# Where the next step's scores stand in the attention steps of a two-layer transformer kernel

## Chip, cores and metric

The kernel runs on one core of one Trainium2 chip. The metric is the device time of one execution in microseconds (us). The median of three runs is given, and beside it stands one profiled execution. TensorE is written PE in the profile, VectorE DVE, ScalarE ACT, GpSimd POOL and SyncE SP.

## The reference, cut to what matters

Two layers, each with four branches (windowed attention A, rotary attention B, differential attention C, a gated linear recurrence D) and a feed-forward part, are followed by a second block with its own sliding-window attention, a state space model and two more feed-forward parts. All is float32; 512 tokens and 16 meta tokens, width 1024. The branches that matter here:

```python
# kind A: windowed, 4 heads of 64, 2 key heads, block of 128 queries
s_b = einsum(qb, kb) * scale + head_bias(rel_b)          # up to 384 keys of the band
s_m = einsum(qb, km) * scale + head_bias(rel_m)          # the 16 meta tokens
p = softmax(concatenate([s_b, s_m, s_sink], axis=-1), axis=-1)
o = einsum(p_b, vb) + einsum(p_m, vm)
# kind B: rotary, all keys
s = where(key_ok, einsum(qblk, k) * scale, MASK_VALUE)   # q, k normalised and rotated
p = softmax(s, axis=-1)
o = einsum(p, v)
```

## The kernel before

**Steps.** The attention of a layer is one list of steps, `att`, in the order of kinds C, A, B. A step is one block of 128 query tokens (the last block of a layer-0 kind has the 16 meta tokens) and one of two pairs of heads. Layer 0 has ten steps of each kind, layer 1 has eight, as it drops the meta tokens' queries. A step of kind C has four cells (head and component), one of A or B has two cells, one for each head. Two successive steps (`i` 0 and 1) share a group, whose output is scaled and stored together. The second block has sixteen steps of kind W, also with two cells.

**What each engine does for one step.** PE: `scores` (L1214; for B and C also L1207, the meta tokens' scores, in PSUM bank 5), which write two PSUM banks per step, A and B in turn banks 0, 1 and 2, 3. DVE: `minima` (L2375) of the negated scores into SBUF, `meta_scores` (L2396). ACT: `exps` (L1816). PE: `turn_probs` for each of the two heads (L1241 for the blocks of 128 keys into bank 4, and with the first head L1238 for the meta tokens into bank 5). ACT: `copy_turned` (L1830, and L1833 for the meta tokens) from PSUM to SBUF. PE: `values` (L1267), in the second step of a group after a spread of the reciprocals (L1253). ACT: `copy_group` (L1839). DVE: `scaled` (L2441).

**The order on PE** is that of the function `attention`, and PE works in program order. In iteration n it takes the scores of step n, the values of step n-2, the first head's transposes of step n-1, then a projection piece if `fills_at` has one for this n, then the second head's transposes of step n-1. A piece (`fill_piece`, L1299 to L1307) is 24 matmuls of the layer's input projection, which use bank 7. Its weights are split into a high and a low part by ACT (L1739) and DVE (L2234) in earlier steps. In five steps from `turn_step` on, `turn_heads` (L1278) transposes the rotated heads of a tile, also in bank 7, behind the second head's transposes. In the second block (`gated=True`) the scores of step n+1 already stand between the piece of other work (`gated_step`) and the second head's transposes.

**Waits that matter.** `turn_probs(c, 0)` waits for both exponentials of the step, `turn_probs(c, 1)` for the copy of the first head's transposes (one bank serves both). `values` waits for the copy of both. `turn_heads` and the next `fill_piece` wait for the copy of the piece. `scores` of a step with meta scores (B, C) waits for the copy of the meta tokens' transposes before it and for DVE's reading of the meta scores before it:

```python
if bank_user(n):
    pe.wait_ge(S["att_min"], bank_user(n))
if c["marked"]:
    if n and att[n - 1]["metas0"]:
        pe.wait_ge(S["att_ptm"], att[n - 1]["metas0"])
```

**Around the steps.** ACT's order in a step is: first exponential, copy of the first head's transposes, copy of a group, second exponential, copy of the piece, copy of the second head's transposes, then weight splits. DVE's minima of step n wait for the second head's transposes of step n-2, whose buffer they write again. In the first steps of A, DVE and POOL also rotate the heads of kind B. From the seventh step of B on (`split_from`) ACT and DVE split the weights and inputs of the gated pieces that follow the attention (L1389 to L1391).

Of the kernel before, what the change touches and what calls it, by code (L numbers as in the profile page):

```python
# [248 lines left out]
def build(nc, ins, out_dram):  # L249
    with ExitStack() as ctx:  # L250
# [456 lines left out]
        att, groups = [], []  # L707
# [52 lines left out]
        for ly in layers:  # L760
            for kind in "CAB":
                first = len(att)
# [48 lines left out]
        def bank_of(c, g):  # L811

            return g if c["kind"] == "C" else 2 * (c["n"] % 2) + g

        def bank_user(n):

            k = n - 1 if n and "C" in (att[n]["kind"], att[n - 1]["kind"]) else n - 2
            return cell_end(k) if k >= 0 else 0
# [232 lines left out]
        def _(pe):  # L1051
# [144 lines left out]
            def scores(c):  # L1196
                n, rows = c["n"], c["rows"]
# [5 lines that stand above are left out]
                    if c["marked0"]:  # L1203
                        pe.wait_ge(S["att_meta"], c["marked0"])
                    q, k = (CQ, MKC) if c["kind"] == "C" else (BQ, MKB)
                    a = c["group"]["a"]
                    mm(PS[0:rows, 5, 256:256 + k.shape[1]], q[c["i"]][:, a:a + rows], k, start=True, stop=True)  # L1207
                for half in range(2):
                    for i in range(len(c["cells"][0]["scores"])):
                        for g, x in enumerate(c["cells"]):  # L1210
                            if x["head"] == half or c["kind"] != "C":
                                col, k = x["scores"][i]
                                if half == 0 or c["kind"] == "C":
                                    last = mm(PS[0:rows, bank_of(c, g), col:col + k.shape[1]], x["q"], k, start=True, stop=True)  # L1214
                    if c["kind"] == "C":
                        last.then_inc(S["att_scores"], 1)
                if c["kind"] != "C":
                    last.then_inc(S["att_scores"], 2)

            def turn_probs(c, j):  # L1220
                n, rows = c["n"], c["rows"]
                if c["kind"] == "C":
                    pe.wait_ge(S["att_mix"], c["mixed0"] + 2)
                else:
                    pe.wait_ge(S["att_exp"], c["cell0"] + (2 if c["metas"] else j + 1))
                if 2 * n + j:
                    pe.wait_ge(S["att_pt"], 2 * n + j)
                of = lambda i: SB[0:rows, c["kept"] + (2 * i if c["kind"] == "C" else i), :]
                if j == 0 and c["metas"]:
                    if c["metas0"]:  # L1230
                        pe.wait_ge(S["att_ptm"], c["metas0"])
                    seen = att[n + 1]["marked0"] + att[n + 1]["marked"] if n + 1 < len(att) else 0
                    if seen and n + 1 < made_scores[0]:
                        pe.wait_ge(S["att_meta"], seen)
                    elif c["marked0"] + c["marked"]:
                        pe.wait_ge(S["att_meta"], c["marked0"] + c["marked"])
                    for i in range(2):
                        turn(PS[0:META, 5, P * i:P * i + rows], of(i)[:, 0:META], ident[0:rows, 0:rows])  # L1238
                for b, (col, v) in enumerate(c["heads"][j]):
                    if v.shape[0] == P:  # L1240
                        last = turn(PS[:, 4, P * b:P * b + rows], of(j)[:, col:col + P], ident[0:rows, 0:rows])  # L1241
                last.then_inc(S["att_turned"], 1)

            def values(c):
                n, rows, g, i = c["n"], c["rows"], c["group"]["n"], c["i"]
                if i and g:
                    pe.wait_ge(S["y_ready"], g)
                if i:
                    pe.wait_ge(S["att_r"], n + 1)
                    for m in range(2):  # L1250
                        for j in range(2):
                            at = 4 * ((n - 1 + m) % 4) + (2 * j if c["kind"] == "C" else j)
                            last = mm(PS[64 * j:64 * j + 64, 6, 256 + P * m:256 + P * m + rows],  # L1253
                                      rcp[0:rows, at:at + 1].to_broadcast([rows, HD]), ident[0:rows, 0:rows],
                                      start=True, stop=True, skip_group_check=True)
                    last.then_inc(S["att_spread"], 1)
                elif g:
                    pe.wait_ge(S["y_ready"], g)
                pe.wait_ge(S["att_pt"], 2 * n + 2)
                if c["metas"]:  # L1260
                    pe.wait_ge(S["att_ptm"], c["metas0"] + 1)
                k = len(c["heads"][0])
                for b in range(k):
                    for j in range(2):
                        v = c["heads"][j][b][1]
                        x = PT[j][:, b, 0:rows] if v.shape[0] == P else PTM[:, j, 0:rows]
                        last = mm(PS[64 * j:64 * j + 64, 6, P * i:P * i + rows], v, x, start=b == 0, stop=b == k - 1,  # L1267
                                  skip_group_check=True)
                last.then_inc(S["att_pv"], 1)
# [15 lines left out]
            def fill_piece(f):  # L1285
                n = f["n"]
                if n:
                    pe.wait_ge(S["fill_read"], n)
                if heads_by[0]:
                    pe.wait_ge(S["b_heads_ready"], heads_by[0])  # L1290
                for ld in f["lds"]:
                    pe.wait_ge(S["w_low"], ld.s + 1)
                a, z = TILES[f["t"]] if f["tokens"] else f["cut"]
                for k in range(KT):
                    xh, xl = HR[:, k, a:z], UR[:, k, a:z]
                    if f["tokens"]:
                        wh, wl = (part(f["lds"][k // 4])[:, k % 4, :] for part in (high, low))
                        out = PS[0:z - a, 7, 0:CG]
                        mm(out, xh, wh, start=k == 0, stop=False)  # L1299
                        mm(out, xh, wl, start=False, stop=False)  # L1300
                        last = mm(out, xl, wh, start=False, stop=k == KT - 1)
                    else:
                        wh, wl = (part(f["lds"][0])[:, k, :] for part in (high, low))
                        out = PS[:, 7, 0:z - a]
                        mm(out, wh, xh, start=k == 0, stop=False)
                        mm(out, wh, xl, start=False, stop=False)
                        last = mm(out, wl, xh, start=False, stop=k == KT - 1)  # L1307
                last.then_inc(S["fill_full"], 1)
                filled_by[0] = n + 1

            made_scores = [0]
# [18 lines left out]
                    mean_tile(b2["n_ssm"], s - MEAN_AT)  # L1330

            def attention(first, end, turns=None, l=0, gated=False):
                if gated:
                    scores(att[first])
                for n in range(first, end + 2):
                    if n < end and not gated:
                        if n == turns:
                            pe.wait_ge(S["b_heads_ready"], NT * (l + 1))
                        scores(att[n])
                        made_scores[0] = n + 1  # L1340
                    if first <= n - 2:
                        values(att[n - 2])
                    if first <= n - 1 < end:
                        turn_probs(att[n - 1], 0)
                    for f in fills_at.get(n, ()) if n < end else ():
                        fill_piece(f)
                    if gated:
                        gated_step(n - first)
                        if n + 1 < end:
                            scores(att[n + 1])  # L1350
                    if first <= n - 1 < end:
                        turn_probs(att[n - 1], 1)
                    if turns and 0 <= n - layers[l]["turn_step"] < NT:
                        turn_heads(l, n - layers[l]["turn_step"])
# [1693 lines left out]
```

## Time and profile before

| | |
|---|---|
| median of three runs | 3123.15 us (3118.74 to 3124.94) |
| profiled execution, its own time | 3124.82 us |
| its span | 3122.8 us |
| PE busy | 3000.0 us, 96% |
| DVE, ACT, POOL busy | 1729.2, 1006.6, 216.9 us |
| mean granted clock of TensorE | 0.978 |
| chain that ended last | PE 89%, DVE 5%, ACT 4%, issue 2% |

The span is the profiled execution from its first to its last instruction. Busy time is what an engine's instructions cover. The chain that ended last is followed back from the last instruction, at each step to what released it; its shares say on which engine time is lost if something is added there. The granted clock is 1.00 when TensorE runs at 2.4 GHz and 0.50 when it runs at 1.2 GHz. Layer 0's kinds A and B lie from 178 to 301 us of the span, layer 1's from 1234 to 1352 us, the second block's attention from 2599 to 2660 us.

### The profile page before, as it was taken

The numbers are of one execution on the slowest core, as the hardware profiler recorded it, in microseconds if no ns is written. First come the engines' busy times: TensorE is split into PE (matmuls) and PEld (weight loads), VectorE is DVE, ScalarE is ACT, GpSimd is POOL, SyncE is SP. The second block draws the span as 40 slices with busy tenths as digits, with TensorE's granted clock in tenths as the row PEclk, the third lists the DMA queues.
The fourth block names the chain that finished last, engine by engine and source line by source line (L and its number), as shares of the span: only waits on it lengthen the run. The fifth ranks groups of instructions, "written<-read, shape, count | busy, mean of one in ns | idle before, by whom it ended". The sixth has DMA issues, their size and how long they took to land.

```text
span 3122.8 us, 51509 instructions
## 1 busy us (share of the span) xinstructions
PE 3000.0 (96%) x21594; PEld 2566.2 (82%) x21594; DVE 1729.2 (55%) x3294; ACT 1006.6 (32%) x1737; POOL 216.9 (7%) x446
## 2 busy tenths in 40 slices
PE   8999999999999999999999999999999899899997
PEld 7877998999999997789998888878888655578886
DVE  4564577457556436547755765657447454543334
ACT  4655232332112336532223222233222305432222
POOL 0130222000000100211210000000000000000000
PEclk9999999999999999989999999999999999999999
DMA  5201111235433321111223443422334311123232
GB/s 185 101 29 35 60 60 61 73 136 171 160 122 123 135 73 42 40 43 61 69 70 143 166 169 130 151 75 94 114 108 150 140 45 38 54 81 106 84 102 73
DMA packets 74494, 302.45 MB, mean 97 GB/s; under 512 B 10729, under 2 KB 11113, under 8 KB 69273
## 3 DMA queue, kind: packets, MB, share of 16 engines
q1 hardware_dynamic: 57880, 230.04, 21.5%
q0 software_dynamic: 16384, 69.13, 6.1%
q8 instruction: 172, 2.82, 0.4%
q14 instruction: 58, 0.47, 0.0%
HBM read 288.51 MB, written 14.63 MB: 97 GB/s over the span
## 4 chain that ended last, share of the span: by engine, by line
PE 89%; DVE 5%; ACT 4%; issue 2%; POOL 0%; DMA 0%; DVEq 0%; SPq 0%; ACTq 0%
PE acc L1066 18%; PE acc L1067 18%; PE acc L1068 18%; PE acc L1389 5%; PE acc L1390 5%; PE acc L1391 5%; PE acc L1085 2%; PE acc L1267 2%; PE acc L1214 1%; ACT temps L1816 1%; PE acc L1617 1%; PE acc L1241 1%; PE acc L1434 1%; PE acc L1455 1%; PE acc L1121 1%
## 5 line engine op out<-in xcount | busy, mean ns | idle before, releaser
L1067 PE MATMUL acc<-normed_r,toep_r 128*128 128x512 f32 (+1 forms) x1808 | 635.4, 351 | 0.0
L1739 ACT ACTIVATE toep_r<-ring 128x1024 fp32r<-128x1024 f32 (+2 forms) x340 | 392.9, 1157 | 695.8 <-PE acc L1068 676.0
L2234 DVE TENSOR_TENSOR ring_r<-ring,toep_r 128x1024 fp32r<-128x1024 f32 (+2 forms) x340 | 458.0, 1348 | 261.3 <-ACT toep_r L1739 261.0
L1067 PEld LDWEIGHTS acc<-normed_r,toep_r 128*128 128x128 f32 x1808 | 340.7, 188 | 45.4 <-issue 0.2
L1066 PE MATMUL acc<-mixed_r,toep_r 128*128 128x264 f32 (+1 forms) x1056 | 342.7, 325 | 0.7 <-DVE normed_r L2217 0.6
L1066 PE MATMUL acc<-work_r,toep_r 128*128 128x512 f32 (+1 forms) x988 | 341.7, 346 | 1.5 <-DVE ring_r L2234 1.4
L1068 PE MATMUL acc<-work_r,ring_r 128*128 128x512 f32 (+1 forms) x988 | 340.9, 345 | 0.0
L1068 PE MATMUL acc<-mixed_r,ring_r 128*128 128x264 f32 (+1 forms) x1056 | 338.8, 321 | 0.0
L1066 PE MATMUL acc<-temps_r,toep_r 128*128 128x512 f32 x752 | 297.6, 396 | 11.5 <-DVE normed_r L2220 8.8
L1067 PE MATMUL acc<-work_r,toep_r 128*128 128x512 f32 (+1 forms) x880 | 307.3, 349 | 0.0
L1389 PE MATMUL acc<-residual_r,toep_r 128*128 128x264 f32 (+1 forms) x1024 | 301.8, 295 | 3.7 <-ACT toep L1956 2.1
L1068 PE MATMUL acc<-temps_r,ring_r 128*128 128x512 f32 x752 | 295.0, 392 | 0.0
L1390 PE MATMUL acc<-normed_r,toep_r 128*128 128x264 f32 (+1 forms) x1024 | 293.1, 286 | 0.0
L1391 PE MATMUL acc<-residual_r,ring_r 128*128 128x264 f32 (+1 forms) x1024 | 291.9, 285 | 0.0
L1066 PEld LDWEIGHTS acc<-mixed_r,toep_r 128*128 128x128 f32 x1056 | 198.8, 188 | 15.9 <-issue 1.0
L1068 PEld LDWEIGHTS acc<-mixed_r,ring_r 128*128 128x128 f32 x1056 | 199.0, 188 | 15.5
L1066 PEld LDWEIGHTS acc<-work_r,toep_r 128*128 128x128 f32 x988 | 185.6, 188 | 26.3 <-issue 2.2
L1389 PEld LDWEIGHTS acc<-residual_r,toep_r 128*128 128x128 f32 x1024 | 196.4, 192 | 10.7 <-issue 2.5
L1068 PEld LDWEIGHTS acc<-work_r,ring_r 128*128 128x128 f32 x988 | 185.6, 188 | 23.9
L1390 PEld LDWEIGHTS acc<-normed_r,toep_r 128*128 128x128 f32 x1024 | 196.6, 192 | 1.7
L1391 PEld LDWEIGHTS acc<-residual_r,ring_r 128*128 128x128 f32 x1024 | 197.0, 192 | 0.0
L1066 PEld LDWEIGHTS acc<-temps_r,toep_r 128*128 128x128 f32 x752 | 141.8, 189 | 50.7 <-issue 11.9
(432 smaller groups left out, 5293.0 us busy)
## 6 DMA issues: line engine op xcount, KB each, us to landing
ring<-in_w_pair SPq DMA_DIRECT2D x176, 512.0 KB, 3.5
ring<-in_w_down SPq DMA_DIRECT2D x64, 704.0 KB, 4.1
ring<-in_w_gb SPq DMA_DIRECT2D x64, 640.0 KB, 3.9
extra<-in_w_ada POOLq DMA_DIRECT2D x18, 1024.0 KB, 5.9
toep<-in_w_ada POOLq DMA_DIRECT2D x18, 1024.0 KB, 6.2
ring<-in_w_tm SPq DMA_DIRECT2D x24, 512.0 KB, 4.3
ring<-in_w_out SPq DMA_DIRECT2D x24, 512.0 KB, 3.5
ring<-in_w_fm SPq DMA_DIRECT2D x20, 512.0 KB, 3.7
```

The source lines that it names most:

```text
L1066: mm(out, wh, xh[:, a:z], start=i == 0, stop=False)
L1067: mm(out, wh, xl[:, a:z], start=False, stop=False)
L1068: last = mm(out, wl, xh[:, a:z], start=False, stop=end)
L1085: last = mm(PB[j.buf][:, s, 0:z - a], (wh, wl, wh)[stage], (xh, xh, xl)[stage][:, a:z], start=stage == 0 and i == 0, stop=stage == 2 and i ...
L1121: last = mm(PB[j.buf][0:j.rows, s, 0:z - a], w, x[:, a:z], start=i == 0, stop=i == len(j.terms) - 1)
L1214: last = mm(PS[0:rows, bank_of(c, g), col:col + k.shape[1]], x["q"], k, start=True, stop=True)
L1267: last = mm(PS[64 * j:64 * j + 64, 6, P * i:P * i + rows], v, x, start=b == 0, stop=b == k - 1, skip_group_check=True)
L1389: mm(out, wh, xh[:, a:z], start=m == 0, stop=False)
L1390: mm(out, wh, xl[:, a:z], start=False, stop=False)
L1391: last = mm(out, wl, xh[:, a:z], start=False, stop=m == len(xs) - 1)
L1739: A(high(ld), slot(ld), ACT.Copy).then_inc(S["w_high"], 1)
L2234: V.tensor_tensor(low(ld), slot(ld), high(ld), ALU.subtract).then_inc(S["w_low"], 1)
```

## The change

For kinds A and B the scores of step n+1 are issued in iteration n, behind the projection piece and ahead of the second head's transposes of step n-1, whenever n and n+1 are of the same kind. The first step of each kind and every step of kind C keep their scores at the head of their own iteration. The second block's steps, all of one kind, get the order that they had. The counter `made_scores`, by which `turn_probs` tells whether the next step's meta scores have been issued, is now set in all stages. Only PE's order changes.

```diff
             def attention(first, end, turns=None, l=0, gated=False):
-                if gated:
-                    scores(att[first])
+                made_scores[0] = first
+
+                def next_scores(n):
+                    scores(att[n])
+                    made_scores[0] = n + 1
+
                 for n in range(first, end + 2):
-                    if n < end and not gated:
+                    if n < end and n >= made_scores[0]:
                         if n == turns:
                             pe.wait_ge(S["b_heads_ready"], NT * (l + 1))
-                        scores(att[n])
-                        made_scores[0] = n + 1
+                        next_scores(n)
+                    kinds = [att[m]["kind"] for m in range(n, min(n + 2, end))]
+                    paired = len(kinds) == 2 and kinds[0] == kinds[1]
                     if first <= n - 2:
                         values(att[n - 2])
                     if first <= n - 1 < end:
@@
                         fill_piece(f)
                     if gated:
                         gated_step(n - first)
-                        if n + 1 < end:
-                            scores(att[n + 1])
+                    if paired and kinds[0] != "C":
+                        next_scores(n + 1)
                     if first <= n - 1 < end:
                         turn_probs(att[n - 1], 1)
```

## Rows read from the trace of the kernel before

**Rows 1.** Windows: start:end, us, busy PE, PEld, DVE, ACT, POOL; clock, DMA.
```profile
179.50:237.20 57.70, 53.04 (x503) 42.51 (x501) 35.84 (x119) 29.84 (x106) 26.09 (x25) 0.94 0.10 35
237.20:301.40 64.20, 58.30 (x573) 45.32 (x572) 31.79 (x93) 40.68 (x100) 0.00 (x0) 1.00 0.13 42
...
2599.00:2660.00 61.00, 51.56 (x372) 27.24 (x360) 29.58 (x131) 41.06 (x135) 0.00 (x0) 1.00 0.11 36
```

**Rows 2.** Waits of PE, layer 0: kind A (179.5 to 237.2), then B.
```profile
PE acc L1241 <- ACT mixed L1830: 2.6, 4, 1.1
PE acc L1278 <- ACT work L1863: 1.2, 3, 0.6
...
PE acc L1278 <- ACT work L1867: 0.4, 1, 0.4
...
PE acc L1241 <- ACT mixed L1830: 3.9, 5, 1.5
```

**Rows 3.** Timeline, PE, second block: start, duration, line, shapes, idle before.
```profile
2630.68 0.44 PE L1241 MATMUL acc<-con,temps 128*128 128x128 f32 x2
2631.71 0.66 PE L1267 MATMUL acc<-mixed,work 128*64 128x128 f32 x8 [0.60 <-ACT mixed L1830]
...
2634.16 0.44 PE L1241 MATMUL acc<-con,temps 128*128 128x128 f32 x2
2634.52 0.66 PE L1253 MATMUL acc<-con,small 128*64 128x128 f32 x8
2635.07 0.33 PE L1267 MATMUL acc<-mixed,work 128*64 128x128 f32 x2
```

**Rows 4.** Timeline, layer 0, step B6: PE and ACT.
```profile
279.38 0.60 PE L1241 MATMUL acc<-con,temps 128*128 128x128 f32 x4
280.76 0.63 PE L1241 MATMUL acc<-con,temps 128*128 128x128 f32 x4 [0.78 <-ACT mixed L1830]
...
280.02 0.60 ACT L1830 ACTIVATE mixed<-acc 128x512 f32<-128x512 f32 x1
280.51 0.36 ACT L1833 ACTIVATE cross<-acc 16x256 f32<-16x256 f32 x1
...
281.50 0.57 ACT L1830 ACTIVATE mixed<-acc 128x512 f32<-128x512 f32 x1
281.97 2.41 ACT L1739 ACTIVATE toep_r<-ring 128x1280 fp32r<-128x1280 f32 x2
```

**Rows 5.** Timeline, PE, layer 0, from step B1's piece to B2's values.
```profile
248.39 0.60 PE L1241 MATMUL acc<-con,temps 128*128 128x128 f32 x4
248.82 0.31 PE L1207 MATMUL acc<-con,work 128*128 128x32 f32 x2
...
250.12 0.33 PE L1267 MATMUL acc<-mixed,work 128*64 128x128 f32 x2
```

**Rows 6.** Timeline, PE, layer 0, step A3.
```profile
198.74 0.49 PE L1241 MATMUL acc<-con,temps 128*128 128x128 f32 x3
199.90 0.52 PE L1241 MATMUL acc<-con,temps 128*128 128x128 f32 x3 [0.67 <-ACT mixed L1830]
200.35 0.29 PE L1214 MATMUL acc<-work 64*128 64x16 f32 x2
```

**Rows 7.** Timeline and window, layer 0, steps A0 and A1.
```profile
181.76 0.58 PE L1241 MATMUL acc<-con,temps 16*128 16x16 f32 x4 [1.07 <-ACT mixed L1830]
...
186.36 0.56 PE L1299 MATMUL acc<-toep_r,residual_r 128*128 128x256 f32 x1
...
182.91 2.35 DVE L2234 TENSOR_TENSOR ring_r<-ring,toep_r 128x1024 fp32r<-128x1024 f32 x2
...
181.70:188.10 6.40, 6.34 (x52) 5.50 (x53) 5.71 (x19) 2.64 (x11) 2.19 (x1) 0.50 0.02 8
```

**Rows 8.** Timeline, PE, layer 1, step A3: the rotated heads.
```profile
1262.30 0.52 PE L1278 MATMUL acc<-con,work 128*128 128x128 f32 x3 [0.24 <-ACT work L1863]
```

**Rows 9.** Timeline, DVE, layer 0, from step B7 to B8.
```profile
286.76 2.89 DVE L2234 TENSOR_TENSOR ring_r<-ring,toep_r 128x1280 fp32r<-128x1280 f32 x2
```

## The prediction, before the result was known

> **What bounds the kernel now.** I read the page first: TensorE is busy 96% of the span and holds 89% of the chain that ended last, so an edit of TensorE's order is paid where TensorE stands still. The change touches kinds A and B of both layers, four stretches of some 60 us each. In layer 0 TensorE is busy 53.0 of 57.7 us in A and 58.3 of 64.2 us in B [rows 1]: some 5 us of each is idle. Next I read who TensorE waits for in these two [rows 2]: in A, 2.6 us in four waits before transposes (L1241) for ScalarE's copy (L1830), and 1.2 and 0.4 us in four before the rotated heads (L1278) for the copy of a projection piece; in B, 3.9 us before L1241. Last comes the timeline, step by step. Below, "A3" is step 3 of kind A, counted from 0. An odd step has the spread of reciprocals (L1253) ahead of its values (L1267); an even step starts its values at once.
>
> **What moves.** In step n TensorE issues today: scores(n), values(n-2), first head's transposes of n-1, a projection piece in most steps, second head's transposes, in five steps the rotated heads. After: scores(n+1) stand behind the piece and ahead of the second head's transposes. No instruction is added or dropped, no DMA is touched. Kind C keeps its order, the first step of A and of B starts as today, and the second block's sixteen steps have this order already, so they stay.
>
> What the scores shielded changes sides. Today their 0.9 to 1.3 us lie between the second head's transposes and the next values, which wait until ScalarE has copied exactly those transposes out of PSUM. After, nothing lies there but, in odd steps, the spread, and in A5 to A9 the rotated heads of the step before.
>
> **The price of the uncovered copy.** The trace has it twice. (a) The second block, which has this order now [rows 3]: second head's transposes start at 2630.68, the values at 2631.71 after 0.60 us idle. That is 1.03 from start to start, against 0.36 where nothing waits (2634.16 to 2634.52). So +0.67 for two blocks in an even step. In the odd step 2634.16 to 2635.07 is 0.91, spread included: 0.1 shorter than 1.03, and less than 0.1 of wait is left beside the spread's 0.5. (b) Between the two heads of a step without a piece. Four blocks, kind B: 279.38 to 280.76 is 1.38 [rows 4], against 0.43 unwaited, 248.39 to 248.82 [rows 5]: +0.95. Three blocks, kind A: 198.74 to 199.90 is 1.16, against 0.45 from 199.90 to 200.35 [rows 6]: +0.71. An odd step loses the spread's 0.5 and the 0.1 from it: +0.34 for four blocks, +0.1 for three. The rotated heads, three more transposes, hide another 0.45: +0.26 for three blocks, +0.22 for two, nothing in odd steps.
>
> **Layer 0, kind A.** Lost: A2 0.67, A3 0.1, A4 0.71, A6 0.26, A8 0.22: 1.96 us. Won: about 1.1 us of scores now cover each of the eight waits of [rows 2], 2.6 + 1.2 + 0.4 = 4.2 us, of which 1.07 are in A0 (181.76) [rows 7]. A0's is not quite whole, for what is late next is the piece of A1, whose weights VectorE splits from 182.91 for 2.35 us, to some 185.2. With 0.14 us for the hand-over it can start at 185.35, against 186.36 now: 1.0. Net -2.1 us.
>
> **Layer 1, kind A** (eight steps, all with pieces). Lost: A1, whose values are kind C's with four blocks, 0.34; A2 0.67; A3 0.1; A4 and A6 0.26 each: 1.63. Won: the waits before the rotated heads of A3 to A6, four times 0.24, of which the first is in [rows 8]: 0.95. Net +0.7.
>
> **Kind B, each layer.** B0 to B5 have no idle time to win back: piece, transposes, scores, values follow without a gap [rows 5]. Lost: B2, B4, B6 0.95 each, B3, B5 0.34 each: 3.53 us. B1's values follow one or two blocks in an odd step: at most 0.1. From B6 on there is no piece. Its wait of 0.78 does not go away: the next scores write the bank in which the 16 meta tokens' transposes lie, and wait for their copy (L1833), which ends at 280.87, later than L1830's at 280.62 [rows 4]. So scores start at 281.01 where transposes start at 280.76 now, and take 1.3 us (248.82 to 250.12, [rows 5]). The second head's transposes end near 282.9, and their copy, at 281.50 now, starts 1.4 us later. Queued behind it on ScalarE without a gap are two weight splits of 2.41 us [rows 4] and the exponentials of B7. Behind those comes the copy of a pair, on which VectorE's scaling, its 2.89 us of splits and the minima of B8 hang [rows 9]. So the last steps end 1.4 to 1.5 us later. B of layer 0: 3.53 + 1.5 = 5.0. Layer 1 has one such step, with splits of the same length behind it: 3.53 + 0.1 + 1.4 = 5.0.
>
> **Sum:** -2.1 + 0.7 + 5.0 + 5.0 = +8.6 us. The profiled execution took 3124.82 us for a span of 3122.8, so it would take 3133.4 for 3131.4. It is 1.67 above the median of the three runs, 3123.15; on the median the sum gives 3131.8 us.
>
> **The clock** is the unknown. TensorE's granted clock is 0.50 (1.2 GHz) for 6.40 us from 181.7, 6.34 of them busy, behind the wait of 1.07 us [rows 7]; the same happens behind the last waits of both B kinds. Such a fall costs up to 3.2 us. In A0 the wait of 1.07 goes, but TensorE then stands 1.6 us for VectorE's splits. If the clock stays up there, the 2.75 us of the fall behind 185.35 cost nothing, and A wins up to 1.4 more, 3.5. If a whole fall starts there, it costs 1.8 more than now, and A wins 0.3. At the ends of the B kinds falls may come earlier, longer or not at all: some 3 us either way. I count all as they are.
> The Trainium skill ("TensorE: Matmul & The Clock Gate", section "A second HAM failure mode: psum-queue depth-cycling") says that frequent small idles between groups of matmuls, made by waits on PSUM, can make the clock oscillate. By that rule every B step, now with a wait of 0.3 to 0.9 us, would be in danger. In this trace it does not hold for waits of that size: the second block's steps have 0.6 us of idle every other step and a granted clock of 1.00 over 61 us [rows 1, 3].
>
> **Rivals.**
> 1. *The waits are hidden after all* (not slower by a measurable amount). For it: VectorE paces A1 and ScalarE the last B steps, so not every wait of TensorE adds up. With B's waits at the bare idle of 0.78 (odd 0.2), tails of 1.0 and A at -3.5, it is 2 x (2.74 + 1.0) + 0.7 - 3.5 = +4.7, and with one fall of the clock fewer about +2: 3125 to 3128. Against it: the start-to-start intervals, which are what the next work feels, are 0.2 us longer than the idle.
> 2. *The clock oscillates* (the page's rule as a mechanism here): two to five more falls of up to 3.2 us each, +15 to +25, 3138 to 3148. Against it stands the row of 61 us at 1.00.
> 3. *Faster*: the values hardly stall on the copy. Were the interval with four blocks 0.9 instead of 1.38 us, the even B steps would lose 0.47, the odd none, the tails 0.5 each and A nothing: 2.8 + 1.0 - 4.1 - 0.95 = -1.3. With the clock up in A0 and the falls at the ends of B gone, some -6.5: near 3116.5. It decides from a copy of 0.2 us, where the rows have 0.57 to 0.60 for four blocks. That the moved scores have no effect at all is excluded, since TensorE keeps the program's order.
>
> **Chances.** Forecast as summed 0.62; rival 1 0.22; rival 2 0.08; rival 3 0.08. 0.2% is 6.2 us, also the distance between the lowest and the highest run before, and about what a measurement of this kernel can tell from no change. So slower by more 0.70, within it 0.22, faster 0.08. The range goes from rival 1's lower part to rival 2's lower edge, 3125.5 to 3138.
>
> **What the profile after would show.** In B2, B4, B6 of both layers idle of some 0.8 us before L1267, released by L1830, in the odd ones 0.2 to 0.3. TensorE's waits for L1830 before L1267 5 to 7 us in the four stretches together, where there are none now. In A the waits before L1278 gone and before L1241 nearly so. The wait of B6 before L1207 instead of L1241. B with pieces 3.5 us longer per layer, its tail 1.5. The second block's stage unchanged. Wrong would be: no idle before L1267; a clock below 1.00 inside B0 to B6; or an A of layer 0 that ends over 3.5 us sooner.

## The result, and the profile of the changed kernel

The changed kernel took 3137.99 us (median of six runs, 3134.62 to 3140.26), the kernel before 3126.30 in six runs (3118.74 to 3129.91). The ratio is 1.004, with a 95% interval from 1.003 to 1.005: slower by 11.7 us by the medians (9.4 to 15.6 by the interval), where 8.6 were forecast. The profiled execution took 3140.13 us for a span of 3138.1, 15.3 more than before. On its page PE is busy 3010.4 us, 10.4 more than before, though it issues the same instructions: part of the loss is not waiting but slower work.

Lines behind the edited function have moved by 5 (L1830 is L1835, L1389 is L1394, L2234 is L2239). As in the prediction, a wait or a loss "in B2" is one in iteration B2, where the values of step B0 stand. The stretches below are named by steps: "B4's values", at which one ends, are the values of step B4, taken in iteration B6. Windows of the changed kernel, columns as in [rows 1]: layer 0's A, its B as far as B4's values, its tail of B (from there to the first gated piece), then the same three of layer 1.

```profile
180.10:237.70 57.60, 55.23 (x527) 43.55 (x525) 37.64 (x123) 31.10 (x110) 26.12 (x25) 0.94 0.11 38
237.70:281.90 44.20, 41.79 (x363) 33.02 (x362) 19.33 (x59) 25.47 (x62) 0.00 (x0) 1.00 0.17 57
281.90:312.80 30.90, 24.37 (x213) 16.15 (x213) 12.49 (x36) 15.72 (x40) 0.00 (x0) 0.72 0.02 6
1242.60:1300.50 57.90, 55.24 (x515) 44.42 (x513) 33.28 (x99) 30.51 (x95) 23.57 (x25) 1.00 0.11 39
1300.50:1346.20 45.70, 43.27 (x372) 33.76 (x372) 19.64 (x59) 25.72 (x59) 0.00 (x0) 1.00 0.16 54
1346.20:1368.10 21.90, 16.09 (x132) 11.32 (x132) 8.34 (x20) 11.28 (x25) 0.00 (x0) 0.75 0.02 8
```

The same six stretches of the kernel before, in one window each:

```profile
178.00:237.20 59.20, 54.54 (x527) 43.62 (x525) 37.04 (x123) 31.34 (x110) 26.09 (x25) 0.94 0.10 37
237.20:277.80 40.60, 40.59 (x363) 33.13 (x362) 18.70 (x56) 25.73 (x62) 0.00 (x0) 1.00 0.17 53
277.80:301.50 23.70, 17.72 (x215) 12.20 (x213) 13.14 (x38) 14.98 (x39) 0.00 (x0) 0.99 0.06 23
1234.10:1290.90 56.80, 54.37 (x515) 44.39 (x514) 32.57 (x99) 31.03 (x94) 23.61 (x25) 1.00 0.12 40
1290.90:1332.50 41.60, 41.60 (x372) 33.84 (x372) 19.01 (x56) 25.84 (x59) 0.00 (x0) 1.00 0.15 49
1332.50:1352.90 20.40, 15.71 (x135) 11.36 (x133) 9.02 (x23) 11.04 (x24) 0.00 (x0) 0.73 0.07 27
```

The differences, from the starts of the instructions at the borders (B4's values start at 277.77 before and at 281.88 after, and so on):

| stretch | forecast | measured in these two profiles |
|---|---|---|
| layer 0, A | -2.1 | -1.58 (59.19 to 57.61) |
| layer 0, B to B4's values | +3.5 | +3.61 (40.55 to 44.16) |
| layer 0, tail of B | +1.5 | +7.19 (23.72 to 30.91) |
| layer 1, A | +0.7 | +1.06 (56.83 to 57.89) |
| layer 1, B to B4's values | +3.6 | +4.05 (41.59 to 45.64) |
| layer 1, tail of B | +1.4 | +1.57 (20.37 to 21.94) |

That is +15.9. Of the rest of the span, the part ahead of layer 0's A is 2.08 longer and the part between the two layers' attention 2.71 shorter, and from layer 1's first gated piece to the end it is 1769.95 us before and 1769.98 after. Five of the six stretches came out within 0.6 us of the forecast. One did not, and its granted clock is 0.72 where it was 0.99. A low stretch of the clock stands at the border behind it in both profiles, so part of what this tail loses comes back in the 2.71 us.

The forecast waits, in PE's timeline of the changed kernel, layer 0, before the values of iteration B3 (odd) and of B4 (even), and the copy that releases the latter on ACT:

```profile
257.61 0.65 PE L1241 MATMUL acc<-con,temps 128*128 128x128 f32 x4
258.19 0.66 PE L1253 MATMUL acc<-con,small 128*64 128x128 f32 x8
258.95 1.09 PE L1267 MATMUL acc<-mixed,work 128*64 128x128 f32 x16
...
265.23 0.66 PE L1241 MATMUL acc<-con,temps 128*128 128x128 f32 x4
266.62 1.09 PE L1267 MATMUL acc<-mixed,work 128*64 128x128 f32 x16 [0.73 <-issue]
...
265.92 0.60 ACT L1835 ACTIVATE mixed<-acc 128x512 f32<-128x512 f32 x1 [1.39 <-PE acc L1241]
```

From start to start the even step takes 1.39 us (forecast 1.38), the odd one 1.34. The idle of 0.73 stands before the values in iterations B2, B4 and B6 of both layers. The profile puts it down to "issue", and one may think that it waits for nothing; but the copy of 0.60 ends at 266.52 and the values start 0.10 later. The doubled copy below settles it.

In layer 0's tail, PE and ACT of the changed kernel, and the window in which the clock is low:

```profile
285.08 0.38 PE L1207 MATMUL acc<-con,work 128*128 128x32 f32 x2 [0.99 <-issue]
...
291.60 0.22 PE L1207 MATMUL acc<-con,work 128*16 128x32 f32 x2 [1.60 <-issue]
...
293.01 1.11 PE L1241 MATMUL acc<-con,temps 128*128 128x128 f32 x4
294.86 1.97 PE L1267 MATMUL acc<-mixed,work 128*64 128x128 f32 x16 [0.73 <-issue]
...
287.63 2.42 ACT L1744 ACTIVATE toep_r<-ring 128x1280 fp32r<-128x1280 f32 x2
```

```profile
292.60:306.10 13.50, 11.78 (x70) 7.25 (x68) 7.31 (x18) 5.48 (x12) 0.00 (x0) 0.50 0.01 1
```

B6's wait stands before the meta scores (L1207), as forecast. B7's is 1.60 us, behind the two weight splits on ACT (2.42 us together). Within a microsecond of its end the granted clock falls to 0.50 (1.2 GHz) and stays there for 13.5 us, 11.8 of them busy: the four transposes take 1.11 us where they take 0.66 at 1.00, the values 1.97 where they take 1.09.

In layer 0's A two of the forecast's details are seen: the wait of A0 is gone, with the next piece waiting for VectorE instead, and the new waits of the even steps are there.

```profile
187.49 0.55 PE L1299 MATMUL acc<-toep_r,residual_r 128*128 128x256 f32 x1 [0.20 <-DVE ring_r L2239]
193.63 0.66 PE L1267 MATMUL acc<-mixed,work 128*64 128x128 f32 x8 [0.52 <-issue]
203.79 0.88 PE L1267 MATMUL acc<-mixed,work 128*64 128x128 f32 x12 [0.63 <-DVE mixed L2446]
```

### The profile page after: what moved, and what is told of

It reads as the page before. It is cut to its first block, busy times and chain, and to the rows that moved or that the text cites. A ratio compares the mean times of both kernels' runs of the same rounds, so it can differ in the third digit from the quotient of the medians.

```text
span 3138.1 us, 51509 instructions
## 1 busy us (share of the span) xinstructions
PE 3010.4 (96%) x21594; PEld 2569.0 (82%) x21594; DVE 1729.7 (55%) x3294; ACT 1006.7 (32%) x1737; POOL 217.2 (7%) x446
## 4 chain that ended last, share of the span: by engine, by line
PE 88%; DVE 5%; ACT 3%; issue 2%; DMA 1%; POOL 0%; SPq 0%; DVEq 0%; ACTq 0%
PE acc L1066 18%; PE acc L1067 18%; PE acc L1068 18%; PE acc L1394 5%; PE acc L1395 5%; PE acc L1396 5%; PE acc L1085 2%; PE acc L1267 2%; PE acc L1214 1%; PE acc L1241 1%; ACT temps L1821 1%; PE acc L1622 1%; PE acc L1439 1%; PE acc L1460 1%; PE acc L1121 1%
## 5 line engine op out<-in xcount | busy, mean ns | idle before, releaser
L2239 DVE TENSOR_TENSOR ring_r<-ring,toep_r 128x1024 fp32r<-128x1024 f32 (+2 forms) x340 | 457.8, 1347 | 261.4 <-ACT toep_r L1744 261.1
L1394 PE MATMUL acc<-residual_r,toep_r 128*128 128x264 f32 (+1 forms) x1024 | 301.3, 294 | 3.7 <-ACT toep L1961 2.1
L1066 PEld LDWEIGHTS acc<-mixed_r,toep_r 128*128 128x128 f32 x1056 | 198.8, 188 | 15.9 <-issue 1.0
L1394 PEld LDWEIGHTS acc<-residual_r,toep_r 128*128 128x128 f32 x1024 | 196.2, 192 | 10.7 <-issue 2.5
```

What stands on the lines that cost most here:

```text
L1066: mm(out, wh, xh[:, a:z], start=i == 0, stop=False)
L1394: mm(out, wh, xh[:, a:z], start=m == 0, stop=False)
L2239: V.tensor_tensor(low(ld), slot(ld), high(ld), ALU.subtract).then_inc(S["w_low"], 1)
```

## The experiments

### Where in the change the loss lies

Four kernels that move the scores in a part of the steps only. The edit is one line, the condition:

```diff
-                    if paired and kinds[0] != "C":
+                    if paired and kinds[0] in "AW":                              # a_only
+                    if paired and kinds[0] in "BW":                              # b_only
+                    if paired and (kinds[0] == "W" or kinds[0] == "B" and n in fills_at):      # b_pieces
+                    if paired and (kinds[0] == "W" or kinds[0] == "B" and n not in fills_at):  # b_tail
```

**Kind A alone.** 

> The moved scores in kind A alone, kind B in its old order. Theory (the edit is paid where TensorE waits for the copy of the second head's transposes): layer 0's A 1.6 us shorter than before and layer 1's A 1.1 us longer, as in the profile after; both B kinds at their old lengths of 64.3 and 62.0 us; in all -0.5 us, not to be told from before. Rival 1 (A's order changes what the clock does behind it, since B's tail in layer 0 comes at another moment): layer 0's tail (from B4's values to the first gated piece) well over its 23.7 us, up to 31, and +5 us or more in all. Rival 2 (the stretches are not independent: A's edit feeds on B's): layer 0's A at its old 59.2 us.

**Kind B alone.** 

> The moved scores in kind B alone, kind A in its old order. Theory: all of the loss lies here. Layer 0's B with pieces 3.6 us longer than before, layer 1's 4.05, layer 1's tail 1.6, layer 0's tail 7.2: 16.4 us, of which the pieces after layer 0's attention gave back 2.7 in the profile after, because a fall of the clock came earlier instead; so +12 to +16 us. Rival (the long tail of layer 0 was a chance of that one profile, not the order's): the tail 1.5 to 2 us longer than its 23.7, and +9 to +11 in all.

**Kind B, the iterations with a piece.** 

> The moved scores in kind B only in iterations that have a projection piece (B0 to B5); from B6 on, and in kind A, the old order. Theory (two separate costs, waits under the pieces and the tail): the stretch with pieces +3.6 and +4.0 us as after, the tails at their old 23.7 and 20.4 us: +7.6 us in all. Rival (the clock falls in the tail because of the waits that B1 to B6 collected before it, not because of the tail's own order): layer 0's tail is still some 5 us longer than before, +12 or more in all.

**Kind B, the iterations without.** 

> The complement: the moved scores in kind B only in iterations without a piece (B6 to B8); everything else in the old order. Theory: the stretch with pieces at its old 40.6 and 41.6 us, layer 0's tail 7.2 us longer with the granted clock at 0.50 inside it, layer 1's 1.6 longer; with 2.7 given back behind layer 0's, +6 us in all. Rival (the order costs the tails 1.5 us each and the clock in layer 0 falls for another reason): tails +1.5 each, the clock at 1.00 until the end of layer 0's tail, +3 in all.

Measured beside 27 runs of the kernel before (median 3126.39):

| kernel | median us | ratio (95%) | L0: A, B, tail | L1: A, B, tail |
|---|---|---|---|---|
| a_only | 3122.56 | 0.9992 (0.9983 to 1.0001) | 58.38, 40.55, 26.52 | 57.88, 41.59, 16.92 |
| b_only | 3134.82 | 1.0033 (1.0021 to 1.0046) | 60.58, 44.18, 25.81 | 56.84, 45.65, 20.90 |
| b_pieces | 3129.78 | 1.0016 (1.0007 to 1.0025) | 60.45, 44.17, 25.11 | 56.83, 45.66, 16.92 |
| b_tail | 3125.04 | 1.0000 (0.9991 to 1.0008) | 59.39, 40.56, 29.23 | 56.83, 41.59, 18.47 |

Four things follow. The loss lies in kind B. B with pieces is 44.17 and 45.66 us wherever its scores are moved, and 40.55 and 41.59 wherever not: this term belongs to the order, to 0.02 us. The tails don't behave so: with the same order they differ by up to 5 us, and with the old order layer 1's is 16.92, not the 20.37 of the first profile. Windows of the tails in a_only (layer 0, layer 1), then in b_tail:

```profile
278.10:304.60 26.50, 20.55 (x214) 14.15 (x212) 13.13 (x38) 14.97 (x39) 0.00 (x0) 0.85 0.06 22
1336.10:1353.10 17.00, 12.21 (x135) 8.64 (x133) 9.04 (x24) 11.04 (x24) 0.00 (x0) 1.00 0.09 34
```

```profile
280.80:310.10 29.30, 22.67 (x215) 15.31 (x213) 13.20 (x39) 15.39 (x40) 0.00 (x0) 0.79 0.05 20
1339.90:1358.30 18.40, 12.52 (x134) 8.56 (x132) 8.98 (x22) 11.08 (x23) 0.00 (x0) 1.00 0.08 30
```

The length follows the clock column. With the clock at 1.00 in both, layer 1's tail takes 16.92 in the old order and 18.47 in the new: the order's own price is 1.55 us. In layer 0, from B4's values to B9's, the kernel before takes 22.27 (277.77 to 300.04) and b_only 24.15 (282.94 to 307.09), both ahead of their fall of the clock: 1.9 us. The forecast had 1.4 and 1.5.

The fourth is that the parts do not add up. By the ratios b_pieces is 5.0 us slower (2.2 to 7.8), b_tail 0 (2.5 at most, where its expectation had 3 or 6), and b_only, which has both edits, 10.3 (6.6 to 14.4), as its rival had it: 9 to 11, with the long tail of layer 0 a chance of one profile. Inside layer 1's tail the clock stays at 1.00 in the one profile of b_pieces and the one of b_tail. It falls there in all six profiles of kernels in which all of B's scores are moved: b_only, the changed kernel twice, and three kernels further below. Such a tail takes 20.9 us or more, against 18.47. Of five profiles with all of B in the old order, two have such a fall too (the kernel before, and its doubled copy below). So the two parts together may bring on a fall that either alone does not. It is not shown: there is one profile of each part alone, and the intervals are so wide that the parts could still add up.

### Does the same program fall at the same place again?

Both kernels, unedited, were profiled once more.

**Before.** 

> The kernel before once more, for a second profile of the same program. Theory (the granted clock inside the tails differs from execution to execution, the waits don't): the stretches without a fall of the clock keep their lengths within 0.1 us (B with pieces 40.6 and 41.6), while the low stretches behind B7's wait of 1.5 us come at another moment or not at all, and a tail differs by 1 us or more from 23.7 or 20.4. Rival (the clock follows from the program): every low stretch of before is at its place again, both tails as they were within 0.2 us.

**Changed.** 

> The changed kernel once more, for a second profile. Theory: B with pieces again 44.2 and 45.6 us, waits of 0.73 us before the values of the even steps again; layer 0's tail not 30.9 us but between 25.3 (the clock at 1.00 throughout: 23.7 and the order's 1.5) and 31. Rival (the order fixes the clock): 30.9 us again, with the granted clock at 0.50 from B7's wait of 1.6 us on.

The kernel before took 3121.88 us, with layer 0's tail at 26.79 and layer 1's at 16.92, against 23.72 and 20.37 in its first profile. The changed kernel took 3135.67, its tails 26.07 and 21.94, against 30.91 and 21.94. B with pieces was 40.56 and 41.59, and 44.16 and 45.65. So the first theory held: the waits are the program's, while the place of a fall differs from one profile to the next, by 3 to 5 us of a tail's time. The two profiles of a kernel may come from different chips, so that a difference between chips is not excluded; but 17 executions of the kernel before on one chip, beside the second profiles, spread from 3119.49 to 3128.69 us. One part goes against the theory: layer 1's tail of the changed kernel came out the same twice. Tails of before's second profile, then of the changed kernel's:

```profile
279.70:306.50 26.80, 20.82 (x215) 14.24 (x213) 13.15 (x38) 15.12 (x39) 0.00 (x0) 0.83 0.06 22
1336.10:1353.10 17.00, 12.21 (x135) 8.63 (x133) 9.04 (x24) 11.03 (x24) 0.00 (x0) 1.00 0.08 33
```

```profile
280.60:306.70 26.10, 18.89 (x213) 12.70 (x213) 12.54 (x36) 15.67 (x40) 0.00 (x0) 0.96 0.02 8
1341.60:1363.60 22.00, 16.12 (x133) 11.40 (x133) 8.41 (x21) 11.38 (x25) 0.00 (x0) 0.75 0.03 9
```

The waits in layer 1's tail are alike where the clock is not. PE's timeline of the changed kernel's second profile, where it falls, and of b_tail, where it doesn't:

```profile
1351.68 0.63 PE L1241 MATMUL acc<-con,temps 128*128 128x128 f32 x4 [1.92 <-ACT mixed L1835]
1353.35 1.97 PE L1267 MATMUL acc<-mixed,work 128*64 128x128 f32 x16 [1.04 <-DVE mixed L2446]
```

```profile
1349.90 0.63 PE L1241 MATMUL acc<-con,temps 128*128 128x128 f32 x4 [1.91 <-ACT mixed L1835]
1351.57 1.09 PE L1267 MATMUL acc<-mixed,work 128*64 128x128 f32 x16 [1.04 <-DVE mixed L2446]
```

### Is the wait before the values the copy's?

ScalarE copies the second head's transposes of kind B twice, in either order:

```diff
+                if j and c["kind"] == "B":
+                    A(aside.rearrange(...)[:, 0:k, 0:rows], PS[:, 4, 0:P * k].rearrange(...)[:, :, 0:rows], ACT.Copy)
                 A(PT[j][:, 0:k, 0:rows], PS[:, 4, 0:P * k].rearrange(...)[:, :, 0:rows], ACT.Copy
                   ).then_inc(S["att_pt"], 1)
```

**In the old order.** 

> The kernel before; in kind B ScalarE copies the second head's transposes twice, the first time into a buffer that nobody reads, so the values are released 0.5 us later (0.49 from start to start of two such copies). Theory (in the old order the scores hide the copy): 1.73 us lie between the start of the transposes and the values where 1.38 are needed, so 0.15 us lost per even step and nothing per odd one; B with pieces 41.0 and 42.0 us. With the tails, where ScalarE is waited for, 1 to 1.5 us longer each, +3 to +4 in all. Rival (ScalarE's time per step is what paces B, the order beside the point): B with pieces some 3 us longer, as in the changed order.

**In the changed order.** 

> The same doubled copy in the changed order. Theory (nothing lies between the transposes and the values now): each of B2 to B6 loses the whole 0.5 us, 2.5 us in B with pieces, which is then 46.7 and 48.2 us, and the waits before the even steps' values grow from 0.73 to 1.2 us; tails 1 to 1.5 longer; +19 us or so against before, +7 to +8 against the changed kernel. Rival (the wait of 0.73 is not for the copy, since the profile names issue for it and not ScalarE): the wait stays 0.73 and the stretch 44.2 us.

In the old order B with pieces was 40.87 and 41.92 us, 0.3 more than before, and the whole 3127.08 (ratio 1.0003, 0.9994 to 1.0013; 3 to 4 us more were expected). In the changed order it was 46.61 and 48.09, 2.45 more than in the changed kernel, and the whole 3142.22 (1.0053, 1.0038 to 1.0068), 15.6 by the medians where 19 were expected. That is 3.9 more than the changed kernel's 11.7, where 7 to 8 were expected and the two stretches alone make 4.9; the whole is no sharper than that. PE and ACT in the changed order, layer 0 (lines moved by one):

```profile
266.93 1.09 PE L1268 MATMUL acc<-mixed,work 128*64 128x128 f32 x16 [1.22 <-issue]
275.01 1.09 PE L1268 MATMUL acc<-mixed,work 128*64 128x128 f32 x16 [0.59 <-ACT mixed L1838]
...
265.75 0.60 ACT L1837 ACTIVATE aside<-acc 128x512 f32<-128x512 f32 x1 [1.40 <-PE acc L1242]
266.24 0.59 ACT L1838 ACTIVATE mixed<-acc 128x512 f32<-128x512 f32 x1
```

The copy is 0.49 later, and the even step's idle grows from 0.73 to 1.22, by 0.49, though it is still called "issue". The odd step now shows 0.59 with the right name. This is the mechanism, shown from both sides: the order, and not ScalarE's time, decides what a copy costs in B with pieces.

### Does the spread of an odd step cover the copy?

```diff
+                    if paired and (kinds[0] == "W" or kinds[0] == "B" and n in fills_at and att[n]["i"] == 0):
```

> The moved scores only in the iterations B0, B2 and B4 of kind B; the values that follow them belong to odd steps and have the spread of the reciprocals ahead; kind A and everything else in the old order. Theory (the spread covers 0.6 of the 0.95 us, as the prediction had it): B1 at most 0.1, B3 and B5 0.34 each: B with pieces +0.7 to +0.8 us, 41.3 and 42.4 us, and the three uneven iterations hold the other 2.8 of the 3.6; within 0.2% of before, +1.5. Rival (each moved step costs the same): +1.8 per layer, 42.4 and 43.4.

B with pieces came out at 41.32 and 42.80: +0.77 and +1.21. The whole took 3123.91 (0.9997, 0.9988 to 1.0006). In layer 1, B3 and B5 cost 0.40 and 0.42 (from values to values: 7.18 to 7.58, 7.17 to 7.59), B1 0.20, and each even step 0.07, which no view explains. B3's pair, in the kernel before and in this one:

```profile
1304.82 1.09 PE L1267 MATMUL acc<-mixed,work 128*64 128x128 f32 x16
1312.00 1.04 PE L1267 MATMUL acc<-mixed,work 128*64 128x128 f32 x16
```

```profile
1305.99 1.09 PE L1267 MATMUL acc<-mixed,work 128*64 128x128 f32 x16
1313.57 1.09 PE L1267 MATMUL acc<-mixed,work 128*64 128x128 f32 x16
```

So the first theory held, with 0.41 where 0.34 was forecast. In the changed kernel an even step costs 1.02 (6.65 to 7.67).

### Can the clock be held up by filling the gaps?

Transposes of the identity go into bank 7, which is idle there, in the changed order. The function is shown without its calls: the first kernel calls it before the values and before the scores in B6 to B9, the second before the values of the even iterations and before the scores in B6 to B9.

```diff
+                def keep_busy(n):
+                    if att[n]["kind"] == "B" and n not in fills_at:    # busy_b: without the second condition
+                        pe.wait_ge(S["fill_read"], filled_by[0])
+                        for b in range(4):
+                            turn(PS[:, 7, P * b:P * b + P], ident, ident)
```

**In the tails.** 

> The changed order, and in the iterations B6 to B9 of both layers four transposes of the identity into the idle bank 7 before the values and four before the scores, 0.6 us of PE work at each place, laid into the gaps. Theory (the falls in the tails come from the gaps there, and PE is not what the tail waits for): the clock stays at 1.00 in both tails, layer 0's tail 25 to 27 us, layer 1's 18.5 to 20; against the changed kernel some -4 us or more, so +5 to +9 against before. Rival 1 (the clock falls for what went before, the pieces): falls in the tails as in the changed kernel, tails as long or up to 4 us longer, +12 to +16. Rival 2 (PE is the tail's bound, the added work is paid in full): each tail 8 times 0.5 = 4 us longer at a clock of 1.00.

**And before the values of every even step of B.** 

> The changed order, with four transposes of the identity into bank 7 before the values of every even step of kind B, whose gap of 0.73 us they fill to 0.3, and before the scores in B6 to B9. Theory (layer 1's tail falls to the clock of 0.50 because of the waits under the pieces and in the tail together, since with either alone it stayed at 1.00): with the gaps under the pieces filled too, layer 1's tail has no fall and takes 18.5 us, not 21.9; B with pieces as in the changed kernel, 44.2 and 45.6; +7 to +9 us against before. Rival (such filling does nothing for the clock, the pieces of idle left suffice, or it is chance): layer 1's tail 21.9 us again with the clock at 0.50 for 13.7 us.

The first took 3134.39 us (1.0028, 1.0016 to 1.0040), the second 3134.59 (1.0027, 1.0017 to 1.0037), 9.7 and 8.0 us over the kernel before by the medians, against the changed kernel's 11.7, but the intervals overlap. Layer 0's tails were 25.74 and 26.23 with a clock of 0.99 and 0.96. Layer 1's was 21.94 in both, as in the changed kernel, in spite of some 1.0 us more PE work; its windows, first kernel and second:

```profile
1343.30:1365.30 22.00, 17.24 (x145) 12.74 (x145) 8.42 (x21) 11.38 (x25) 0.00 (x0) 0.75 0.03 10
```

```profile
1342.40:1364.40 22.00, 16.99 (x141) 12.26 (x141) 8.41 (x21) 11.38 (x25) 0.00 (x0) 0.75 0.03 11
```

So in these profiles the theory of each expectation fell in layer 1. Waits of 1.36 and 1.04 us (first kernel), 1.48 and 1.04 (second) were left there in the iteration behind B6, and the clock fell during the latter, as in the changed kernel. In the first kernel:

```profile
1353.37 0.63 PE L1241 MATMUL acc<-con,temps 128*128 128x128 f32 x4 [1.36 <-ACT mixed L1845]
1355.03 1.97 PE L1267 MATMUL acc<-mixed,work 128*64 128x128 f32 x16 [1.04 <-DVE mixed L2456]
```

This profile is that of the slowest of the first kernel's seven executions, 3137.02 us. Three of them took 3126.59, 3127.05 and 3129.78, each below all seven of the changed kernel's (3134.62 at the least). What the clock did in those three no profile shows, so it is not settled that such filling in the tails gains nothing.

That PE is not the tail's bound is seen in layer 0, whose 25.74 with 28 more transposes stand beside b_only's 25.81. Rival 2 falls with that. What makes the clock fall in layer 1 stays open.

### A version that beats both

The moved scores in A's even iterations alone, where the values that follow have the spread ahead of them.

```diff
+                    if paired and (kinds[0] == "W" or kinds[0] == "A" and att[n]["i"] == 0):
```

> The moved scores in kind A alone, and there only in even iterations, so that the values which then follow the second head's transposes are those with the spread of the reciprocals between; kind B in its old order. Theory: the waits of iterations A0, A4, A6 and A8 (1.07, 0.78, 0.67, 0.35 us) are covered, of which A0's is handed on to the piece's splits in part, and the odd iterations lose 0.1 us each: layer 0's A -1.5 to -2.4 us, layer 1's A -0.2; in all some -2 us, at the edge of what can be told from before. Rival (the covered waits come back as waits for VectorE or the piece in the next iteration): layer 0's A at 58.4 us or more, nothing in all.

It took 3119.44 us against 3124.72 (17 runs), ratio 0.9986, 0.9977 to 0.9995: faster by 0.14%, 4.4 us (1.6 to 7.2). The expectation named two outcomes and the stretches lie nearer the rival: layer 0's A is 58.60 and layer 1's 57.01. Covered waits come back one step on:

```profile
184.93 0.39 PE L1241 MATMUL acc<-con,temps 16*128 16x16 f32 x4 [0.22 <-ACT mixed L1835]
188.58 0.55 PE L1299 MATMUL acc<-toep_r,residual_r 128*128 128x256 f32 x1 [0.87 <-DVE ring_r L2239]
...
218.29 0.52 PE L1278 MATMUL acc<-con,work 128*128 128x128 f32 x3 [0.88 <-ACT work L1868]
```

Layer 0's A in the old order took 59.19 to 60.58 in seven profiles, so the stretch itself accounts for 0.6 to 2.0 us. The rest of the 4.4, if it is there, is not accounted for. Nor is it shown that the even iterations are what gains: a_only, with all of A's scores moved, had 0.9992 (0.9983 to 1.0001), and the two intervals overlap.

## Why the prediction was right or wrong, step by step

**The mechanism** (right). The scores no longer cover the copy of the second head's transposes; the doubled copy shows it in both orders.

**The price of the uncovered copy** (right, a little low). Even step in B 0.95 forecast, 1.02 measured; odd 0.34 against 0.41. "B1 at most 0.1" was -0.18 in layer 0 and +0.20 in layer 1. B with pieces is 3.61 and 4.05 against 3.5 and 3.6.

**Kind A** (right in kind, the gain sized too large). Layer 0: -2.1 forecast, where its own terms, 1.96 lost and 4.13 won, give -2.17. A mean of 57.9 over six profiles with A's scores moved (57.44 to 58.42) and 59.8 over the seven without is -1.9. But in three of the seven, those of 60.45 to 60.58 us, the clock over A is 0.92 at most, and in the other four (59.19 to 59.40) 0.94, as in all six. At the same clock A wins 1.4, and the other 0.5 is the clock's. Layer 1: +0.7 against +1.06, with idles of 0.52 and twice 0.30 us before the even steps' values. The waits before the rotated heads (L1278) were said to go; 0.3 us of them are left in layer 0 and 0.4 in layer 1.

**The tails of B** (the step that failed: "I count all as they are"). Their own price was nearly right: 1.9 and 1.55 at full clock against 1.5 and 1.4. But the falls of the clock were counted at nothing on balance. They were also read too small: the forecast priced each by A's low stretch of 6.40 us, up to 3.2 us, and put the others behind the last waits. In layer 1 of the same trace the clock falls inside the tail, 11 us ahead of its end, and stays low to 1358.9:

```profile
1341.90:1352.90 11.00, 8.49 (x59) 6.32 (x59) 4.49 (x7) 3.04 (x9) 0.00 (x0) 0.50 0.00 0
```

The means over the profiles say that the clock was not neutral:

| | old order, 6 profiles | new order, 4 profiles |
|---|---|---|
| layer 0's tail | 25.4 (23.72 to 26.79) | 28.0 (25.81 to 30.91) |
| layer 1's tail | 17.5 (16.92 five times, 20.37) | 20.8 (18.47 to 21.94) |
| layer 0's tail and all up to layer 1's A | 957.5 (956.0 to 958.6) | 959.2 (957.5 to 960.8) |
| layer 1's tail and all behind it | 1785.8 (1783.5 to 1790.3) | 1790.1 (1787.0 to 1792.0) |

(old: before twice, a_only, b_pieces, a_even, b_even; new: changed twice, b_only, b_tail). That is 5.9 us for both tails where 2.9 were forecast, and 3.45 of it is there at full clock: the clock's part is some 2.5 us. The last two rows count in what a low stretch across a tail's end gives back: 1.7 and 4.3 us, together 6.0. So the sum stands, but layer 0 has no more than its own 1.9 in it, and the clock's part lies in layer 1. The clock fell inside layer 1's tail in three of the four with the new order there and in one of the six with the old. Four and six profiles of so scattered a quantity don't fix its size.

**The sum.** -1.9 + 1.06 + 3.6 + 4.05 + 5.9 = +12.7, beside a measured 11.7 (9.4 to 15.6). Of the 4.1 by which this sum exceeds the forecast of 8.6, the tails' clock is 2.5, the undersized waits 0.5, the tails' own price 0.5, and the two A's 0.6.

**The base.** The forecast of 3131.8 stood on a median of three runs, 3123.15. Six runs of the same kernel give 3126.30, and the 27 beside the first experiments 3126.39. So 3.15 of the 6.2 us between 3131.8 and 3137.99 are the base's and not the change's. 3137.99 lies at the very edge of the range, which ended at 3138.0.

**The rivals.** *Hidden after all* is excluded by 44.16 against 40.55. *Faster* would need a short copy; it has 0.60. *The clock oscillates* had a part of the truth: there was more low clock in the tails, but none among B0 to B6, where the granted clock is 1.00 in both layers with 0.73 us of idle in every other step. The rule of the Trainium skill ("TensorE: Matmul & The Clock Gate", section "A second HAM failure mode: psum-queue depth-cycling") speaks of small repeated idles. By the traces here, such idles alone left the clock up for 44 us, and in the changed kernel it fell where waits of 1.0 to 1.9 us stood close together.

**What the profile was to show.** Idle before B2's, B4's, B6's values: 0.8 said, 0.73 seen, under the name "issue". Of odd steps no idle is listed, and 0.4 is lost nevertheless: the idle is smaller than the loss. Waits before the values: 5 to 7 us said, 6.9 seen in twelve waits, besides three (0.6, 0.7, 1.0) that the profile gives to VectorE and of which the kernel before has two. B6's wait before L1207: seen.

## What to carry to other kernels

Before an instruction is moved, list what it covers behind it as well as what it would cover ahead: here 1.1 us of scores covered either the projection's copy or the probabilities', and in B with pieces only the latter was waited for. Move it in those steps alone where the uncovered one has another cover (A's even iterations, a ratio of 0.9986 here, where the whole change gave 1.004 and all of A 0.9992). Compare stretches between the same two instructions, with the clock column beside them, before a whole is explained: here three stretches (layer 1's A and both B with pieces) repeat to 0.1 us in the same order, layer 0's A scatters by up to 1.4, and the tails by up to 5. Profile a kernel more than once where its executions fall into groups, and put a forecast on more than three runs of the base.

## What the runs showed of the hardware

- The granted clock of one program differs by place from one profile to the next: layer 0's tail of the unedited kernel before had it at 0.99 once and at 0.83 once, 23.7 and 26.8 us. The same waits (1.91 and 1.92, then 1.04 us) met a fall of the clock in one kernel and none in another.
- Idles of 0.73 us in every other step left the clock at 1.00 through the 44 and 46 us of B with pieces, and idles of 1.22 and 0.59 us left it there through 46.6 and 48.1 us in the kernel with the doubled copy:

```profile
236.60:283.20 46.60, 41.75 (x363) 33.01 (x363) 19.85 (x62) 27.63 (x67) 0.00 (x0) 1.00 0.17 57
1299.90:1348.00 48.10, 43.25 (x370) 33.75 (x371) 20.11 (x61) 27.91 (x64) 0.00 (x0) 1.00 0.15 54
```

- Filling 0.4 us of such gaps with transposes raised PE's busy time by 1 us in layer 1's tail and left both its length and its clock of 0.75 as they were, in one profile of each of two kernels.
- A wait for a semaphore can be listed as "issue": the 0.73 us became 1.22 when the copy came 0.49 later. In the same kernel the odd step's 0.59 us got the copy's name.
